# Query square sums in the DeltaNet stage: TensorE transposes squared on ScalarE in place of GpSimd squares and matmuls with a column of ones

## The chip, the cores and the metric

The kernel runs on one core of a Trainium2 chip. Its time is the device time of one execution in microseconds (us). Two numbers are used: the median of several runs, and the span of one profiled execution, from its first to its last instruction. The profile tells what each engine did in that one execution: PE is TensorE (matmuls, with PEld its weight loads), DVE is VectorE, ACT is ScalarE, POOL is GpSimd, SP is SyncE, which issues DMAs.

## The reference

One step of a decoder with two layers: a gated DeltaNet layer with a dense channel mixer, then a sliding-window attention layer with an expert mixer. 512 prompt tokens and 8 sample tokens pass through both. The change touches only the DeltaNet mixer of the prompt, and there the norm of the queries:

```python
def l2_norm(x):
    xf = x.astype(jnp.float32)
    return xf * lax.rsqrt(jnp.sum(xf * xf, axis=-1, keepdims=True) + EPS)
...
    q = l2_norm(q.reshape(Bn, T, A_HEADS, A_DK)) * (A_DK ** -0.5)
    k = l2_norm(k.reshape(Bn, T, A_HEADS, A_DK))
...
        o = (jnp.einsum('bhck,bhkv->bhcv', qi * jnp.exp(gi)[..., None], S)
             + jnp.einsum('bhij,bhjv->bhiv', attn, v_new))
...
    o = rms_norm(o, o_norm) * jax.nn.silu(zf)
```

The output of a token is linear in its query, so the norm of the query can be applied late: the kernel computes with unnormed queries and folds the sum of their squares into the norm of the output. That sum, one number for each token and head, is what is computed in another way here.

## The kernel before

The whole program is written out by engine, with semaphores between the engines. Its stages follow each other: input projection, the DeltaNet stage (`delta_phase`, from about 218 to 440 us of the span), output projection, dense mixer, attention, experts.

`delta_phase` goes through the 512 prompt tokens in NCH = 4 chunks of C = 128. The 8 heads are two groups, g = 0 and 1, of HL = 4 heads. Almost every step exists twice, once for each group, and is one instruction over 4 heads, or 4 matmuls. Every engine runs through its steps in the order in which the code lists them. The loop over chunks n inverts a triangular matrix in five levels (s = 2, 4, 8, 16, 32, two sets of 64x64 matmuls each, with ScalarE's copy of Y between them and VectorE's subtraction behind them), and between the levels stand steps that prepare chunk n + 1 ("prep") and steps that carry the state of chunk n - 1 on ("chain"). A class `Lane` counts the steps: `done(ins, who, n, step)` makes an instruction raise a semaphore, `after(eng, n, who=step)` makes an engine wait until that step is done.

PSUM has 8 banks, 4 for each group. Bank 3 of a group, `bank(g, 3)`, is used for one preparation step after another: decay matmuls, key transposes (`k_tok`), key scores (`kk`), query scores (`qk`), value transposes (`v_tok`), and last the square sums of the queries (`ssq`). Before the decay matmuls of the next chunk may write the bank, PE waits for VectorE's step `bq`, which reads the sums.

The path of the square sums of chunk n in the kernel before:

- GpSimd, `squares` (L803, tensor_tensor on L805): the queries `tokens(0, g, n)` times themselves into the buffer `SQ`, 128x512 for each group, issued early, behind the level s = 2 of the chunk before.
- PE, `query_sums` (L951 to L955): behind `solve_keys` and ahead of `recall`, for each of 4 heads a matmul with that head's squares as weights and one column of ones as the moving operand, result 128x1.
- VectorE, `queries` (L1368): scales the queries in place by the decay; it has to come after whatever reads the unscaled queries. Then `query_sums` (L1377): `bq` = (sum + EPS) * EPS * DK, read from PSUM, 128x4. Then `new_values` (L1394), two instructions for each group that wait for PE's `recall`.

Who waits for `bq`: PE's `decay` of the next chunk (L928), VectorE's own `sums_out`, and for the last chunk (n = NCH - 1) PE's `sample_scores` (L1054), which waits for `bq` of group 0 on L1057 because it writes that group's bank 3. `sample_scores` is a long run of small matmuls for the sample tokens, placed behind `recall` of chunk 2, ahead of the last chunk's levels.

In the trace, buffers have the names of the memory that they lie in: VectorE's `tt` helper is L1337, PE's transposes are L902 (`turn`), its 128x128 products L907 (`full`), its 64x64 products L913 (`blocks`). `SQ` of group 0 and 1 is `over_w_hi` and `over_w_lo`, the queries, keys and values are `qkv`, the small factors `delta_small`, the constant tile with identity and ones is `cst`, PSUM is `P`.

Of the kernel before, what the change touches and what calls it, by code (L numbers as in the profile page):

```python
# [17 lines left out]
ALU = mybir.AluOpType  # L18
# [9 lines left out]
AH, DK = 8, 128  # L28
# [657 lines left out]
def delta_phase(nc, c, io, L, sp_next):  # L686
# [17 lines left out]
    by_level = lambda *names: [f"{name}{s}" for s in LEVELS for name in names]  # L704
    prep, inv, chain = ([Lane(c, f"{what}{g}", steps) for g in range(2)] for what, steps in (
        ("prep", {"pe": ["decay", "k_tok", "kk", "qk", "v_tok", "ssq"],
                  "act": ["e_last", "e_left", "e_tok", "e_row", "k_copy", "e_attn", "sq_k", "root"],
                  "dve": ["left", "diff", "LT", "c", "attn", "VP", "q_dec", "bq"],
                  "pool": ["sq_q", "mask", "LT"]}),
        ("inv", {"pe": ["E1"] + by_level("Y", "XW") + ["Y64", "W64"],  # L710
                 "act": by_level("Y") + ["Y64", "F11", "F22", "F12"],
                 "dve": ["W1", "X1"] + by_level("XW"),
# [56 lines left out]
    with nc.Block() as block:  # L769
# [21 lines left out]
        def _(pool):  # L791
# [8 lines left out]
                prep[g].done(nc.gpsimd.affine_select(out=big("AT", g, n), in_=big("AT", g, n), compare_op=ALU.is_ge, fill=low, base=0,  # L800
                                                     pattern=[[0, HL], [1, C]], channel_multiplier=-1), "pool", n, "mask")

            def squares(g, n):  # L803
                prep[g].after(pool, n - 1, pe="ssq")
                prep[g].done(nc.gpsimd.tensor_tensor(big("SQ", g), tokens(0, g, n), tokens(0, g, n), ALU.mult), "pool", n, "sq_q")  # L805

            def scale(g, n):
                prep[g].after(pool, n, dve="c")
                LTc, LT12, cc = big("LTc", g), big("LT12", g, n), small("c", g, n)
# [43 lines left out]
                nc.gpsimd.tensor_tensor(k_mask[:, k], k_row[:, k].unsqueeze(1).broadcast_to([128, TS, 128]),  # L853
                                        cols(c, CPLACE, TS).unsqueeze(2).broadcast_to([128, TS, 128]), ALU.mult).then_inc(s_masked, 1)

            for step in (squares, mask, scale):
                for g in both:
                    step(g, 0)
            for s in (1, 2):
# [2 lines left out]
            for n in range(NCH):  # L862
                more, last = n + 1 < NCH, n == NCH - 1
                for s in LEVELS:
                    if s < 32:
                        for g in both:
                            part(g, n, 2 * s)
                    if more and s == 2:
                        for g in both:
                            squares(g, n + 1)  # L870
                    if more and s == 4:
                        for g in both:
                            mask(g, n + 1)
                    if s == 8:
                        for g in both:
                            decay_state(g, n)
                    if n == 0 and s == 16:
                        pool.wait_ge(edge_stored, 48)
                        for pad in pads:
                            nc.gpsimd.memset(pad, 0.0).then_inc(s_cleared, 1)  # L880
                    if n == 1:
                        fade_sample(LEVELS.index(s))
                    if n == 2 and s < 16:
                        fade_sample(5 + LEVELS.index(s))
                    if last and s >= 16:
                        mask_keys(s // 32)
                if more:
                    for g in both:
                        scale(g, n + 1)
                        part(g, n + 1, 1)  # L890
                if n:
                    for g in both:
                        weigh_F(g, n)
                if more:
                    for g in both:
                        part(g, n + 1, 2)

        @block.tensor
        def _(pe):
# [49 lines left out]
                prep[g].done(turn(bank(g, 3), tokens(2, g, n)), "pe", n, "v_tok")  # L949

            def query_sums(g, n):  # L951
                prep[g].after(pe, n, dve="VP", pool="sq_q")
                for h in range(HL):
                    ins = pe.matmul(c.P[:, 4 * g + 3, h:h + 1], big("SQ", g)[:, h], ones[:, 0:1], start=True, stop=True)
                prep[g].done(ins, "pe", n, "ssq")  # L955

            def first(g, n):
                inv[g].after(pe, n, pool="E1")
# [216 lines left out]
        def _(act):  # L1175
# [30 lines left out]
            def key_root(g, n):  # L1206
                prep[g].after(act, n, act="sq_k")
                prep[g].done(nc.scalar.activation(small("ssk", g, n), small("ssk", g, n), ACT.Sqrt, bias=cols(c, CEPS, 1)),
                             "act", n, "root")

            def level(g, n, s):
                inv[g].after(act, n, pe=f"Y{s}")
                inv[g].done(copy(big("Y", g), half(g, 0, 0)), "act", n, f"Y{s}")
# [34 lines left out]
            def edges(part):  # L1248
                act.wait_ge(edge_turned, part + 1)
                copy(edge_rows[:, part * 512:(part + 1) * 512], c.P[0:11, (4, 5, 6, 0, 1, 2)[part]]).then_inc(edge_read, 1)  # L1250
# [34 lines left out]
                    step(g, 0)  # L1285
            for part in range(3, 6):
                edges(part)
            for n in range(NCH):
                more, last = n + 1 < NCH, n == NCH - 1
                for s in LEVELS:  # L1290
                    for g in both:
                        level(g, n, s)
                    if more and s == 2:
                        for g in both:
                            decays(g, n + 1)
                    if n == 0 and s == 2:
                        nc.scalar.activation(L.s_decay[:], L.gb_sample[:, 0:AH * TS], ACT.Exp).then_inc(s_decays, 1)
                    if s == 4 and n:
                        for g in both:
                            square_out(g, n - 1)  # L1300
                    if more and s == 8:
                        for step in (keys, mask):
                            for g in both:
                                step(g, n + 1)
                    if more and s == 16:
                        key_sums(0, n + 1)
                    if s == 16 and n:
                        for g in both:
                            root_out(g, n - 1)
                    if more and s == 32:  # L1310
                        key_sums(1, n + 1)
                        for g in both:
                            key_root(g, n + 1)
                    if n == 0 and s == 4:
                        sample_rows()
                    if last and s == 2:
                        sample_take()
                    if last and s == 4:
                        sample_squares()
                for g in both:  # L1320
                    join(g, n)
                if n == 0:
                    sample_roots()
                for g in both:
                    corners(g, n)
                if n:
                    for g in both:
                        solve_keys(g, n)
            for g in both:
                square_out(g, NCH - 1)  # L1330
            for g in both:
# [3 lines left out]
        def _(dve):  # L1335
# [30 lines left out]
                prep[g].done(tt(big("AT", g, n), bank(g, 3), big("AT", g, n), ALU.mult), "dve", n, "attn")  # L1366

            def queries(g, n):  # L1368
                prep[g].after(dve, n, pool="sq_q")
                prep[g].done(tt(tokens(0, g, n), tokens(0, g, n), big("ER", g), ALU.mult), "dve", n, "q_dec")  # L1370

            def values(g, n):
# [2 lines left out]
                prep[g].done(tt(big("VP", g, n), bank(g, 3), per_head(small("ssk", g, n)), ALU.mult), "dve", n, "VP")  # L1375

            def query_sums(g, n):  # L1377
                prep[g].after(dve, n, pe="ssq")
                prep[g].done(nc.vector.tensor_scalar(small("bq", g, n), c.P[:, 4 * g + 3, 0:HL], EPS, EPS * DK, ALU.add, ALU.mult),
                             "dve", n, "bq")  # L1380

            def first(g, n):
# [110 lines left out]
            for n in range(NCH):  # L1493
# [40 lines left out]
                    if last and s == 32:  # L1534
                        sample_update(0)
                if more:
                    for step in (query_scores, first, values, queries, query_sums):
                        for g in both:
                            step(g, n + 1)
                if last:  # L1540
# [1 line left out]
                        sample_update(q)  # L1542
                for g in both:
                    new_values(g, n)
            sample_update(5)
            for g in both:
                add_state(g, NCH - 1)
# [1670 lines left out]
```

## Time and profile before

| what | us |
|---|---|
| median of 3 runs | 1588.41 (1588.24 to 1590.96) |
| the profiled execution | 1588.98 |
| its span | 1587.2 |
| PE busy | 1479.2 (93%) |
| DVE busy | 900.5 (57%) |
| ACT busy | 648.6 (41%) |
| POOL busy | 208.7 (13%) |

1.8 us of the profiled execution lie outside its span, and it is 0.57 us longer than the median. Busy times count what an engine executes, not its waits. PE is busy nearly always, so its steps set the time as long as it doesn't stand waiting; the other engines matter where PE waits for them. The granted clock of TensorE is 1.00 where it runs at 2.4 GHz and 0.50 where it runs at 1.2 GHz.

### The profile page before, as it was taken

To read this page: it belongs to the slowest core of one execution; us is meant where nothing else is said; L and a number is where in the kernel's file an instruction comes from. 1 tells how busy PE (TensorE), PEld (TensorE's weight loads), DVE (VectorE), ACT (ScalarE), POOL (GpSimd) and SP (SyncE) were. 2 spreads that over 40 slices of the span, in tenths; PEclk is the share of its full clock that TensorE was granted. 3 is DMA by queue.
4 is the path that set the end of the run, shared out by engine and by line. 5 is a ranking of instruction groups with operands and counts; after the bars stand their busy time and mean duration, and the time that the engine had idled before them with its cause. 6 is when DMAs were issued, how large, how long until landed. Compare 5 with 4: busy or idle time off the path is not lost. (4 is left out here: it accounts for less than half of the span.)

```text
span 1587.2 us, 31920 instructions
## 1 busy us (share of the span) xinstructions
PE 1479.2 (93%) x13294; PEld 1320.5 (83%) x13294; DVE 900.5 (57%) x1197; ACT 648.6 (41%) x1108; POOL 208.7 (13%) x217
## 2 busy tenths in 40 slices
PE   6999989899889999999999998879879999999994
PEld 6999978889889999999999997458867777777773
DVE  5676534755465443444444754543366777676776
ACT  5343534442143222222232413552434565665661
POOL 0111024554011000000011100220011000000002
PEclk8999999999889999999999997889879999999997
DMA  6678240000352323231334530005137888888886
GB/s 177 226 267 280 78 120 2 2 2 3 107 156 72 106 79 106 79 103 57 91 91 131 151 103 21 1 1 134 72 121 240 287 289 294 290 295 268 272 284 239
DMA packets 169741, 226.13 MB, mean 142 GB/s; under 512 B 11272, under 2 KB 134689, under 8 KB 169545
## 3 DMA queue, kind: packets, MB, share of 16 engines
q1 hardware_dynamic: 160246, 191.44, 38.7%
q0 software_dynamic: 8512, 30.48, 5.3%
q10 hardware_dynamic: 862, 2.50, 0.4%
q8 instruction: 88, 1.44, 0.4%
q14 instruction: 33, 0.27, 0.1%
HBM read 188.78 MB, written 37.88 MB: 143 GB/s over the span
## 5 line engine op out<-in xcount | busy, mean ns | idle before, releaser
L276 DVE TENSOR_TENSOR w_lo<-w_raw,w_hi 128x2048 fp32r<-128x2048 f32 (+1 forms) x71 | 153.9, 2172 | 91.4 <-ACT w_hi L268 91.4
L268 ACT ACTIVATE w_hi<-w_raw 128x2048 fp32r<-128x2048 f32 (+1 forms) x71 | 128.1, 1810 | 124.0 <-PE P L221 118.5
L221 PE MATMUL P<-xf_hi,w_hi 128*128 128x260 f32 x704 | 141.8, 282 | 2.0 <-DVEq L1764 1.2
L221 PE MATMUL P<-xf_hi,w_lo 128*128 128x260 f32 x704 | 141.9, 283 | 0.0
L221 PE MATMUL P<-xf_lo,w_hi 128*128 128x260 f32 x704 | 141.7, 283 | 0.0
L221 PEld LDWEIGHTS P<-xf_hi,w_hi 128*128 128x128 f32 x704 | 108.5, 188 | 2.6 <-issue 1.4
L221 PEld LDWEIGHTS P<-xf_hi,w_lo 128*128 128x128 f32 x704 | 108.5, 188 | 0.0
L221 PEld LDWEIGHTS P<-xf_lo,w_hi 128*128 128x128 f32 x704 | 108.2, 188 | 0.0
L221 PE MATMUL P<-xa_hi,w_hi 128*128 128x260 f32 x512 | 104.1, 285 | 2.7 <-DVE xa_lo L319 2.7
L221 PE MATMUL P<-xa_hi,w_lo 128*128 128x260 f32 x512 | 104.1, 285 | 0.0
L221 PE MATMUL P<-xa_lo,w_hi 128*128 128x260 f32 x512 | 103.9, 285 | 0.0
L2095 PE MATMUL P<-w_hi,xb_hi 128*128 128x512 f32 x344 | 102.6, 401 | 0.0
L1848 DVE TENSOR_TENSOR w_lo<-raw_more_moe,w_hi 128x1024 fp32r<-128x1024 f32 x64 | 77.1, 1223 | 42.6 <-ACT w_hi L1842 41.9
L1848 DVE TENSOR_TENSOR w_lo<-w_raw,w_hi 128x1024 fp32r<-128x1024 f32 x64 | 77.1, 1223 | 25.8 <-ACT w_hi L1842 24.4
L1842 ACT ACTIVATE w_hi<-raw_more_moe 128x1024 fp32r<-128x1024 f32 x64 | 66.1, 1054 | 44.6 <-DMA raw_more_moe<-in_moe_w_gu_dram 19.1
L221 PEld LDWEIGHTS P<-xa_hi,w_hi 128*128 128x128 f32 x512 | 80.0, 191 | 2.8 <-issue 2.8
L1842 ACT ACTIVATE w_hi<-w_raw 128x1024 fp32r<-128x1024 f32 x64 | 67.0, 1059 | 33.1 <-DMA w_raw<-in_moe_w_gu_dram 18.2
L221 PEld LDWEIGHTS P<-xa_hi,w_lo 128*128 128x128 f32 x512 | 79.9, 191 | 0.0
L221 PEld LDWEIGHTS P<-xa_lo,w_hi 128*128 128x128 f32 x512 | 79.7, 190 | 0.0
L2095 PEld LDWEIGHTS P<-w_hi,xb_hi 128*128 128x128 f32 x344 | 62.0, 188 | 19.1 <-issue 6.2
L221 PE MATMUL P<-f_hi,w_hi 128*128 128x260 f32 x352 | 70.9, 283 | 0.0
L221 PE MATMUL P<-f_hi,w_lo 128*128 128x260 f32 x352 | 70.8, 282 | 0.0
(553 smaller groups left out, 3320.5 us busy)
## 6 DMA issues: line engine op xcount, KB each, us to landing
raw_more_moe<-in_moe_w_gu_dram SPq DMA_DIRECT2D x64, 512.0 KB, 5.3
w_raw<-in_moe_w_gu_dram SPq DMA_DIRECT2D x64, 512.0 KB, 5.4
w_raw<-in_dense_w_gu_dram SPq DMA_DIRECT2D x44, 512.0 KB, 4.5
expert_out<-zeros POOLq DMA_DIRECT2D x40, 512.0 KB, 4.1
w_raw<-in_a_w_in_dram SPq DMA_DIRECT2D x32, 512.0 KB, 5.0
raw_more_moe<-in_moe_w_down_dram SPq DMA_DIRECT2D x32, 512.0 KB, 4.8
w_raw<-in_moe_w_down_dram SPq DMA_DIRECT2D x32, 512.0 KB, 4.7
w_raw<-in_dense_w_down_dram SPq DMA_DIRECT2D x16, 384.0 KB, 4.0
```

Of the source, the lines that this page charges most:

```text
L221: ins = nc.tensor.matmul(out[:, b], w, x[:, b * HALF:(b + 1) * HALF], start=(first and n == 0), stop=(last and n == 2))
L268: ins = nc.scalar.activation(hi, raw, ACT.Copy)
L276: ins = nc.vector.tensor_tensor(lo, raw, hi.bitcast(F32), ALU.subtract)
L1842: nc.scalar.activation(self.hi[m % 6], self.raw[s], ACT.Copy).then_inc(self.hi_done, 1)
L1848: nc.vector.tensor_tensor(self.lo[m % 6], self.raw[m % len(self.raw)], self.hi[m % 6].bitcast(F32), ALU.subtract).then_inc(self.lo_done, 1)
L2095: ins = pe.matmul(c.P[:, bank + b], a[:, t], x[:, b * 512:(b + 1) * 512], start=(t == 0 and x is w_hi and a is hi), stop=(t == KT - 1 and ...
```

## The change

The squares on GpSimd and the matmuls with ones go away. In their place PE transposes the queries of the chunk (4 transposes for each group, into bank 3, token on the partitions), and ScalarE takes the transposes from PSUM and squares them, with its accumulator adding each row up: 4 activations for each group, which write the sum into the small tile `bq`. VectorE then works on that small tile.

```diff
-                  "act": ["e_last", "e_left", "e_tok", "e_row", "k_copy", "e_attn", "sq_k", "root"],
+                  "act": ["e_last", "e_left", "e_tok", "e_row", "k_copy", "e_attn", "sq_k", "root", "sq_q"],
-                  "pool": ["sq_q", "mask", "LT"]}),
+                  "pool": ["mask", "LT"]}),
...
@block.gpsimd
-            def squares(g, n):
-                prep[g].after(pool, n - 1, pe="ssq")
-                prep[g].done(nc.gpsimd.tensor_tensor(big("SQ", g), tokens(0, g, n), tokens(0, g, n), ALU.mult), "pool", n, "sq_q")
-
...
-            for step in (squares, mask, scale):
+            for step in (mask, scale):
...
-                    if more and s == 2:
-                        for g in both:
-                            squares(g, n + 1)
...
@block.tensor
             def query_sums(g, n):
-                prep[g].after(pe, n, dve="VP", pool="sq_q")
-                for h in range(HL):
-                    ins = pe.matmul(c.P[:, 4 * g + 3, h:h + 1], big("SQ", g)[:, h], ones[:, 0:1], start=True, stop=True)
-                prep[g].done(ins, "pe", n, "ssq")
+                prep[g].after(pe, n, dve="VP")
+                prep[g].done(turn(bank(g, 3), tokens(0, g, n)), "pe", n, "ssq")
...
@block.scalar
+            def query_sums(g, n):
+                prep[g].after(act, n, pe="ssq")
+                for h in range(HL):
+                    ins = nc.scalar.activation(big("SQ", g)[:, h], bank(g, 3)[:, h], ACT.Square, accum_out=small("bq", g, n)[:, h:h + 1])
+                prep[g].done(ins, "act", n, "sq_q")
+
...
+            for g in both:
+                query_sums(g, 0)
             for n in range(NCH):
...
                 if n:
                     for g in both:
                         solve_keys(g, n)
+                if more:
+                    for g in both:
+                        query_sums(g, n + 1)
...
@block.vector
             def queries(g, n):
-                prep[g].after(dve, n, pool="sq_q")
+                prep[g].after(dve, n, pe="ssq")
...
             def query_sums(g, n):
-                prep[g].after(dve, n, pe="ssq")
-                prep[g].done(nc.vector.tensor_scalar(small("bq", g, n), c.P[:, 4 * g + 3, 0:HL], EPS, EPS * DK, ALU.add, ALU.mult),
+                prep[g].after(dve, n, act="sq_q")
+                prep[g].done(nc.vector.tensor_scalar(small("bq", g, n), small("bq", g, n), EPS, EPS * DK, ALU.add, ALU.mult),
...
-                    for step in (query_scores, first, values, queries, query_sums):
+                    for step in (query_scores, first, values, queries):
                         for g in both:
                             step(g, n + 1)
...
                 for g in both:
                     new_values(g, n)
+                if more:
+                    for g in both:
+                        query_sums(g, n + 1)
```

For chunk 0, VectorE's order stays as it was (`query_sums` directly behind `queries`); for chunks 1 to 3 it moves behind `new_values` of the chunk before.

VectorE at the end of the chunk n = 2, before. The `qkv` rows are `queries`, the L1379 rows are `query_sums` (`delta_small_2628` is group 0, `2629` group 1), the four rows behind them are `new_values`, the last is the addition to the state:

```order
L1337 TENSOR_TENSOR qkv<-qkv,delta_own 128x4x128 [waits prep0_pool]
L1337 TENSOR_TENSOR qkv<-qkv,over_w_lo 128x4x128 [waits prep1_pool]
L1379 TENSOR_SCALAR delta_small_2628<-P 128x4 [waits prep0_pe]
L1379 TENSOR_SCALAR delta_small_2629<-P 128x4 [waits prep1_pe]
L1337 TENSOR_TENSOR delta_own<-P,delta_small_2628 128x512 [waits chain0_pe]
L1337 TENSOR_TENSOR delta_own<-P,delta_small_2628 128x512 [waits prep0_act,chain0_pe]
L1337 TENSOR_TENSOR over_w_lo<-P,delta_small_2629 128x512 [waits chain1_pe]
L1337 TENSOR_TENSOR over_w_lo<-P,delta_small_2629 128x512 [waits prep1_act,chain1_pe]
L1337 TENSOR_TENSOR delta_own<-delta_own,P 128x512 [waits chain0_pool,chain0_pe]
```

The same place after the change, where VectorE's helper is L1339 and `query_sums` L1381:

```order
L1339 TENSOR_TENSOR qkv<-qkv,delta_own 128x4x128 [waits prep0_pe]
L1339 TENSOR_TENSOR qkv<-qkv,over_w_lo 128x4x128 [waits prep1_pe]
L1339 TENSOR_TENSOR delta_own<-P,delta_small_2628 128x512 [waits chain0_pe]
L1339 TENSOR_TENSOR delta_own<-P,delta_small_2628 128x512 [waits prep0_act,chain0_pe]
L1339 TENSOR_TENSOR over_w_lo<-P,delta_small_2629 128x512 [waits chain1_pe]
L1339 TENSOR_TENSOR over_w_lo<-P,delta_small_2629 128x512 [waits prep1_act,chain1_pe]
L1381 TENSOR_SCALAR delta_small_2628<-delta_small_2628 128x4 [waits prep0_act]
L1381 TENSOR_SCALAR delta_small_2629<-delta_small_2629 128x4 [waits prep1_act]
L1339 TENSOR_TENSOR delta_own<-delta_own,P 128x512 [waits chain0_pool,chain0_pe]
```

The two `bq` rows have moved behind the four of `new_values` and wait for ScalarE; `queries` waits for PE and no longer for GpSimd.

PE at the same place after the change. The L895 rows are the new transposes, L1005 is `recall`, L1049 and L1056 are the first instruction and the body of `sample_scores`:

```order
L895 MATMUL P<-cst,qkv 128x128 [waits prep0_dve]
L895 MATMUL P<-cst,qkv 128x128 x3
L895 MATMUL P<-cst,qkv 128x128 [waits prep1_dve]
L895 MATMUL P<-cst,qkv 128x128 x3
L1005 MATMUL P<-delta_front,delta_own 128x128 [waits chain0_dve,chain0_act]
L1005 MATMUL P<-delta_front,delta_own 128x128 x3
L1005 MATMUL P<-delta_front,over_w_lo 128x128 [waits chain1_dve,chain1_act]
L1005 MATMUL P<-delta_front,over_w_lo 128x128 x3
L1049 MATMUL P<-cst 128x512 [waits prep0_dve,sample_faded,sample_padded]
L1056 MATMUL P<-s_state,over_raw 8x128 x128
```

The transposes stand where the matmuls with ones stood, and the order on PE is the same otherwise; L1049 still waits for a VectorE step of group 0's preparation, which is `bq` of chunk 3.

## Rows read from the trace of the kernel before

**Rows 1.** The page: busy time by engine, and the granted clock in 40 slices.

```profile
PE 1479.2 (93%) x13294; PEld 1320.5 (83%) x13294; DVE 900.5 (57%) x1197; ACT 648.6 (41%) x1108; POOL 208.7 (13%) x217
PEclk8999999999889999999999997889879999999997
```

**Rows 2.** Timeline, PE, chunk 1 to 2: start us, busy us, instruction, [idle before].

```profile
319.00 1.04 PE L902 MATMUL P<-cst,qkv 128*128 128x128 f32 x8
319.96 0.68 PE L964 MATMUL P<-cst,over_w_hi 64*64 64x64 f32 x16
...
322.93 0.95 PE L954 MATMUL P<-cst,over_w_hi 128*128 128x1 f32 x8
...
324.63 1.14 PE L1014 MATMUL P<-delta_own 128*128 128x128 f32 x8
...
327.85 1.13 PE L907 MATMUL P<-delta_own 128*128 128x128 f32 x8
...
329.71 1.95 PE L932 MATMUL P<-cst,G_tok 128*128 128x128 f32 x16
```

**Rows 3.** Timeline, the same stretch on DVE, POOL and ACT.

```profile
322.89 0.68 DVE L1337 TENSOR_TENSOR qkv<-qkv,delta_own 128x512 f32<-128x512 f32 x1
...
323.17 0.99 POOL L824 TENSOR_TENSOR over_w_lo<-over_pair,levels 128x256 f32<-128x256 f32 x1 [0.16 <-PE P L907]
323.49 1.22 DVE L1337 TENSOR_TENSOR qkv<-qkv,over_w_lo 128x512 f32<-128x512 f32 x1
...
325.81 1.29 DVE L1337 TENSOR_TENSOR delta_own<-P,delta_small 128x512 f32<-128x512 f32 x2 [0.84 <-PE P L1014]
...
327.32 0.85 ACT L1177 ACTIVATE over_pair<-P 128x256 f32<-128x256 f32 x2 [3.60 <-PE P L913]
```

**Rows 4.** Timeline, chunk 2 to 3, PE and DVE around `sample_scores`.

```profile
366.81 0.95 PE L954 MATMUL P<-cst,over_w_hi 128*128 128x1 f32 x8
...
368.52 0.34 DVE L1379 TENSOR_SCALAR delta_small<-P 128x4 f32<-128x4 f32 x2
...
369.69 1.29 DVE L1337 TENSOR_TENSOR delta_own<-P,delta_small 128x512 f32<-128x512 f32 x2 [0.84 <-PE P L1014]
370.48 1.12 PE L1058 MATMUL P<-cst 1*128 1x512 f32 x2
...
371.53 7.17 PE L1065 MATMUL P<-s_state,over_raw 128*8 128x128 f32 x256
```

**Rows 5.** Timeline, chunk 0 to 1, PE and ACT.

```profile
279.09 1.05 PE L954 MATMUL P<-cst,over_w_hi 128*128 128x1 f32 x8 [1.62 <-DVE delta_own L1337]
...
281.69 0.85 ACT L1177 ACTIVATE over_pair<-P 128x256 f32<-128x256 f32 x2 [7.38 <-PE P L913]
...
282.22 2.05 PE L907 MATMUL P<-delta_own 128*128 128x128 f32 x8
...
285.61 1.95 PE L932 MATMUL P<-cst,G_tok 128*128 128x128 f32 x16
```

**Rows 6.** Timeline, PE before chunk 0's levels.

```profile
239.87 1.05 PE L954 MATMUL P<-cst,over_w_hi 128*128 128x1 f32 x8 [2.03 <-DVE delta_own L1337]
...
242.34 1.12 PE L913 MATMUL P<-over_w_hi,delta_own 64*64 64x64 f32 x16
```

**Rows 7.** Timeline, ACT: first and last of 8 squares with accumulator from PSUM.

```profile
292.06 0.27 ACT L1238 ACTIVATE delta_own<-P 128x128 f32<-128x128 f32 x1
...
293.97 0.26 ACT L1238 ACTIVATION_READ_ACCUMULATOR over_w_lo<-P 128x1 f32 x1
```

**Rows 8.** Busy time by stretch: us, then busy (count) by engine, PE clock, DMA share, GB/s.

```profile
242.00:244.00 2.00, 2.00 (x34) 1.99 (x34) 0.16 (x1) 0.38 (x1) 1.99 (x3) 0.50 0.00 0
282.00:284.00 2.00, 1.89 (x12) 1.81 (x9) 1.62 (x3) 1.74 (x3) 2.00 (x2) 0.50 0.04 8
306.00:308.00 2.00, 0.73 (x20) 0.74 (x22) 2.00 (x4) 0.22 (x2) 0.51 (x1) 1.00 0.00 0
```

**Rows 9.** Timeline, PE, inside chunk 1.

```profile
307.27 0.68 PE L913 MATMUL P<-over_w_hi,delta_own 64*64 64x64 f32 x16 [2.28 <-DVE over_w_hi L1337]
```

## The prediction

> **What bounds the kernel now.** I read the page first: PE is busy for 93% of the span, at a clock near full [rows 1], so a step that PE no longer makes is a gain as long as PE doesn't wait for something new. Then I read the timeline of the DeltaNet stage from one square-sum step to the next, on all engines. There are four such places: before the levels of chunk 0, and at the ends of chunks 0, 1 and 2. The reader is to look there for three things: how long PE takes from the start of the square-sum matmuls to its next step, who reads the bank behind it, and what else PE is about to wait for. At the ends of chunks 1 and 2, PE goes from L907 through L954 to L1014 without a gap [rows 2]: it is the bound there. At the end of chunk 0 and before chunk 0 it starts L954 late, because VectorE's values come late (1.62 and 2.03 us of waiting) [rows 5, 6]; the change doesn't touch that. GpSimd is busy 13% of the time [rows 1], and none of its squares holds up PE, so what it loses is worth nothing by itself.
>
> **The change part by part.**
>
> *PE.* The 8 matmuls with ones of both groups appear as 16 passes and take PE from 322.93 to 324.63, 1.70 us [rows 2]. Eight transposes of 128x128 (the values' own, L902) take it from 319.00 to 319.96, 0.96 us for both groups, in one pass each [rows 2]. So each place gives back 1.70 - 0.96 = 0.74, about 0.75 us, where PE is the bound. That an operation with 128 moving columns is cheaper than one with a single column is what the rows say: what both pay is the weight load, and the matmul in fp32 pays it twice. The Trainium skill, "TensorE: Matmul & The Clock Gate", Part 4: PE-mode transpose, gives about 275 ns for a 128x128 transpose inside a kernel; if each took that in sequence, eight would take 2.2 us, and each place would lose 0.5 us instead. The trace speaks against that reading: the busy time of one overlaps the next.
>
> *GpSimd.* Eight squares of about 1 us go. They stand beside other work; worth zero, and at the ends of chunks the next E products may start a little earlier, which nobody waits for.
>
> *ScalarE.* Eight squares with accumulator from PSUM take from 292.06 to 294.23, 2.17 us for both groups [rows 7]. They stand behind `solve_keys` and ahead of the copy of Y of the first level, which `level_two` and `add_state` on PE wait for.
>
> *End of chunk 1.* ScalarE has been free since 327.32 - 3.60 = 323.72 [rows 3]; the first transposes are done by about 323.5; the squares run from 323.75 to 325.9. The Y copy is wanted at 327.32 - 0.75 = 326.57. It is covered with 0.65 us to spare. VectorE: `queries` starts at 322.89 now [rows 3], ahead of L954 on PE; in future it waits for the transposes, until about 323.6 and 324.1. Its two instructions then meet GpSimd's E products. Where they met before, the second took 1.22 us and not 0.68, and GpSimd's 0.99 [rows 3]. If the two alternate, as there, `queries` ends at about 325.8, and the four instructions of `new_values`, which start at 325.81 now [rows 3] at some 0.6 us each, end near 328.3; the two `bq` follow until 328.6 (0.34 us for both [rows 4]). PE wants `bq` for the decay matmuls at 329.71 - 0.75 = 328.96 [rows 2], and `new_values` for L907 at 327.85 - 0.75 = 327.10, when group 0's first is done. Nothing new waits: -0.75 us.
>
> *End of chunk 2.* The same, until `sample_scores`. It waits for `bq` of group 0. Now `bq` is done by 368.86 and PE starts L1058 at 370.48, right behind `recall` [rows 4]. After the change `bq` stands behind `new_values`, and that waits for `recall`. By the rows: PE would be ready at 370.48 - 0.75 = 369.73. VectorE can start `new_values` at 369.69 - 0.75 = 368.94 if `queries` is over by then, and at about 369.7 if it alternates with GpSimd as above. Four instructions of some 0.6 us and `bq` (0.17) make 2.6 to 2.7 us: `bq` of group 0 is ready at 371.6 or at 372.4. L1058 starts then, 1.1 or 1.9 us later than now. All of it is on the path: nothing else is under way, and PE has `sample_scores` (7.17 us) next [rows 4]. I take the upper value, +1.9, because at the same place one chunk earlier the rows show the encounter with GpSimd. The Trainium skill, "SBUF — State Buffer", section "SBUF: two separate sides", states that a VectorE operation with two SBUF inputs and a GpSimd operation lock each other out for the whole of an instruction. The 1.22 us of the row agree; by that rule the place costs +1.9, and without it +1.1.
>
> *End of chunk 0.* The levels' first step would start 0.75 us earlier, but ScalarE comes later. VectorE's instructions of this size follow each other by 0.6 us (323.49 - 322.89 [rows 3]), so group 1's transposes have their values at 279.09 + 0.6 = 279.7, and the squares run from about 279.85 to 282.0, and the Y copy, now at 281.69 [rows 5], starts at 282.0. L907, now at 282.22, waits for it until 282.4. So +0.1 us here, where the 0.75 could have been: the cover is gone by 1 us. L907 then runs, now as before, at half clock: 3.39 us for both groups from 282.22 to 285.61 [rows 5], with a granted clock of 0.50 [rows 8], against 329.71 - 327.85 = 1.86 us at full [rows 2]. If that half-speed stage went away, 1.5 us would be gained. PE has had a wait of 1.62 us and one-column matmuls just before it [rows 5]; afterwards it would have the same wait, real transposes, and a new wait of about a microsecond. I can't tell from the rows, and leave the stage as it is.
>
> *Before chunk 0.* L954 starts at 239.87 and the levels at 242.34, 2.47 us later [rows 6]; the transposes of group 0 start at the same time, those of group 1 when its values are there, 0.6 us later at 240.47, and end half a microsecond later: the levels start at 240.95, 1.4 us earlier. The clock is at 0.50 at 242 [rows 8]. If it comes back at the same moment as before, the 1.4 us pulled ahead run at half speed and 0.7 are kept; if the whole stage shifts, 1.4. ScalarE's squares (2.17 us from 240.5) end near 242.7, and the `bq` for the decay matmuls is ready about then; PE has two sets of 64x64 matmuls until then. I take -1.4.
>
> *Sum:* -1.4 + 0.1 - 0.75 + 1.9 = -0.15 us. Its bounds: -0.15 - 0.8 (no encounter in chunk 2) = -0.95, and +0.7 (prologue at half) = +0.55. Behind the stage PE runs on as before: what is gained or lost moves everything behind it. Against the profiled execution (1588.98) that is 1588.8, and against the median, which is 0.57 lower, 1588.41 - 0.15 = 1588.3 us.
>
> **The rivals.**
>
> *Faster: half-speed stages shorten.* PE now has two such stages beside the changed steps, one around 242 and one around 282 [rows 8]. Each is worth about 1.5 us by the difference above (3.39 against 1.86). One gone: 1588.3 - 1.5 = 1586.8. Both, or one and a later one that starts at another moment: 1585.3. For it: real matmul work takes the place of one-column matmuls. Against it: the waits ahead of them stay. Chance 0.22 for one, 0.09 for two or more.
>
> *The wait of `sample_scores` doesn't bind.* If VectorE got through `new_values` sooner, the third place would give -0.75 and not +1.9: 1588.3 - 2.65 = 1585.7. Against it: the order of VectorE puts four instructions that need `recall` ahead of `bq`, and `recall` is what PE finishes last. Chance 0.05.
>
> *Transposes no cheaper.* If transposes of queries cost what the matmuls did, the chunk 1 place gives 0, the place before chunk 0 about 0.7 less, and the third still ends with `bq`: 1588.3 + 0.75 + 0.7 + 0.2 = 1590.0. Against it: the same instruction on the same tile shape is in the trace. Chance 0.04.
>
> *Slower: the new wait brings the clock down under `sample_scores`.* PE would stand for 2 to 2.7 us just ahead of 7.17 us of matmuls [rows 4]. If the clock fell to half and stayed there for all of it, up to 7.2 us would be added: 1595.5; if for half of it, 3.6: 1591.9. It decides from the point at which the wait is long enough for the clock to fall. Against it: a wait of 2.28 us ended at 307.27 [rows 9], and the clock is 1.00 in 306 to 308 with PE busy 0.73 of 2 us [rows 8]. Chance 0.09, and 0.07 for more than 3.2 us.
>
> **How the numbers follow.** Forecast 1588.3 with a chance of 0.51 (its own range 1587.3 to 1589.5), the others as given. A measurement of this kernel tells about 0.2% (3.2 us) from no change: below 1585.2, above 1591.6. Faster needs two stages of half speed gone, or one and the missing wait: 0.10. Slower needs the clock under `sample_scores`: 0.07. The rest, 0.83, is within. The range from 1585.3 to 1591.0 takes in one stage more or less, both bounds of the third place and the execution-to-execution spread of the runs before (2.7 us).
>
> **What would show it.** In the profile after: from the first transposes of the queries to L1005 about 0.95 us (right) or 1.7 (wrong); on ScalarE, eight squares in about 2.2 us directly behind the WK copies; between L1005 and L1049 a wait of 1.9 to 2.7 us for VectorE's small tile, the largest single change; at the end of chunk 0 the Y copy behind the squares without a gap; in the stretches at 242 and 282 the clock. The prediction would be wrong if that wait were missing or the clock under L1056 were 0.50.

## The result and the profile after

The kernel after took 1593.11 us (median of 20 runs, 1587.61 to 1597.48), the kernel before 1589.01 us (median of 20, 1586.46 to 1590.96). The ratio is 1.0026, with a 95% interval of 1.0017 to 1.0034: slower, by some 4 us. The profiled execution of after took 1594.36 us, with a span of 1592.6 us; that of before 1588.98, with a span of 1587.2.

The page of after, busy time by engine and granted clock, beside [rows 1]:

```profile
PE 1480.7 (93%) x13262; PEld 1318.2 (83%) x13262; DVE 901.8 (57%) x1197; ACT 656.0 (41%) x1172; POOL 200.2 (13%) x209
PEclk8999999999789999999999997789879999999997
```

PE's busy time rose by 1.5 us although it runs 32 passes fewer: the modelled time of a matmul grows with a lower clock. The answer is in the places that the change touches. The timeline of after, PE (start us, busy us, instruction, idle before in brackets), ahead of chunk 0's levels, beside [rows 6]:

```profile
239.79 1.25 PE L895 MATMUL P<-cst,qkv 128*128 128x128 f32 x8 [2.03 <-DVE delta_own L1339]
240.97 1.07 PE L906 MATMUL P<-over_w_hi,delta_own 64*64 64x64 f32 x16
...
245.59 0.68 PE L906 MATMUL P<-over_pair,over_w_hi 64*64 64x64 f32 x16
```

The levels start at 240.97 and not at 242.34, 1.4 us sooner. The clock, too, is back sooner (0.88 in 244 to 246 us, where it was 0.50, and 0.53 in 246 to 248): `level_two` starts at 245.59, 2.35 us ahead of before. The end of chunk 0, on PE, DVE and POOL, beside [rows 5]:

```profile
276.56 1.90 POOL L843 TENSOR_TENSOR s_state<-s_state,s_decay 128x1024 f32<-128x1024 f32 x1
276.59 0.67 DVE L1339 TENSOR_TENSOR over_w_lo<-P,delta_small 128x512 f32<-128x512 f32 x1
276.72 1.25 PE L895 MATMUL P<-cst,qkv 128*128 128x128 f32 x8 [1.62 <-DVE delta_own L1339]
277.42 1.59 DVE L1339 TENSOR_TENSOR qkv<-qkv,delta_own 128x512 f32<-128x512 f32 x1 [0.15 <-PE P L895]
...
278.68 0.91 POOL L820 TENSOR_TENSOR delta_own<-over_w_hi,levels 128x256 f32<-128x256 f32 x1 [0.22 <-PE P L906]
...
278.93 1.21 DVE L1339 TENSOR_TENSOR qkv<-qkv,over_w_lo 128x512 f32<-128x512 f32 x1
...
280.06 1.28 DVE L1339 TENSOR_TENSOR delta_own<-P,delta_small 128x512 f32<-128x512 f32 x2
280.79 1.16 PE L900 MATMUL P<-delta_own 128*128 128x128 f32 x8 [1.74 <-DVE delta_own L1339]
...
281.99 2.07 PE L900 MATMUL P<-over_w_lo,over_w_hi 128*128 128x128 f32 x8
...
286.49 0.68 PE L906 MATMUL P<-over_pair,over_w_hi 64*64 64x64 f32 x16
```

`fade_sample(0)` on GpSimd (L843, the fading of the sample state), 1.90 us long, stands on top of the first of VectorE's two `queries`, and the E product behind it (L820) on top of the second: they take 1.59 and 1.21 us in place of 0.68 each. `new_values` comes late, PE waits 1.74 us, and the clock goes to half behind that wait (2.07 us for a step that takes 1.06 at full). The lead is down to 1.00 us. The end of chunk 1, beside [rows 2] and [rows 3]:

```profile
322.01 1.04 PE L895 MATMUL P<-cst,qkv 128*128 128x128 f32 x8
322.88 1.06 PE L1005 MATMUL P<-delta_own 128*128 128x128 f32 x8
...
327.88 1.95 PE L925 MATMUL P<-cst,G_tok 128*128 128x128 f32 x16
```

Eight transposes take PE 0.87 us. The place goes as forecast: the decay matmuls start 1.83 us ahead of before where the values' transposes were 0.92 ahead. The end of chunk 2, beside [rows 4]:

```profile
364.99 1.04 PE L895 MATMUL P<-cst,qkv 128*128 128x128 f32 x8
365.86 1.06 PE L1005 MATMUL P<-delta_front,delta_own 128*128 128x128 f32 x8
366.75 1.06 PE L1005 MATMUL P<-delta_front,over_w_lo 128*128 128x128 f32 x8
370.27 1.55 PE L1049 MATMUL P<-cst 1*128 1x512 f32 x2 [2.46 <-DVE delta_small L1381]
371.76 10.00 PE L1056 MATMUL P<-s_state,over_raw 128*8 128x128 f32 x256
```

and VectorE in the same stretch:

```profile
366.44 1.21 DVE L1339 TENSOR_TENSOR qkv<-qkv,over_w_lo 128x512 f32<-128x512 f32 x1
367.58 1.28 DVE L1339 TENSOR_TENSOR delta_own<-P,delta_small 128x512 f32<-128x512 f32 x2
368.78 1.27 DVE L1339 TENSOR_TENSOR over_w_lo<-P,delta_small 128x512 f32<-128x512 f32 x2
369.97 0.23 DVE L1381 TENSOR_SCALAR delta_small<-delta_small 128x4 f32<-128x4 f32 x2
```

PE stands for 2.46 us ahead of `sample_scores`, since `bq` is behind the four instructions of `new_values`. Then `sample_scores` takes 10.00 us for its large step, not 7.17. The windows of after give PE's busy time with its count, the granted clock, DMA share and GB/s:

```profile
368.00:370.00 2.00, 0.00 (x0) 1.00 0.00 0
370.00:372.00 2.00, 1.73 (x10) 0.69 0.03 8
372.00:374.00 2.00, 2.00 (x44) 0.50 0.00 0
374.00:376.00 2.00, 2.00 (x47) 0.50 0.00 0
376.00:378.00 2.00, 2.00 (x52) 0.60 0.00 0
```

Behind a stretch in which PE did nothing, the clock is at its lower level (1.2 GHz) for most of the step: 44 matmuls in 2 us in place of the 84 of full speed. The next level step starts at 381.99, against 378.94 before: 3.05 us behind. The remaining 2.3 us of the 5.4 between the two profiled executions come later, where no instruction changed. 1.4 of them come before the output projection, which starts at 447.83 against 443.37; there the half-speed stretches lie otherwise (granted clock 0.67 in 400 to 426 us, before 0.74).

### The profile page after: what moved, and what is told of

The parts are those of the page before. It is cut to its first block and busy times, and to the rows that moved or that the text cites. A ratio compares the mean times of both kernels' runs of the same rounds, so it can differ in the third digit from the quotient of the medians.

```text
span 1592.6 us, 31904 instructions
## 1 busy us (share of the span) xinstructions
PE 1480.7 (93%) x13262; PEld 1318.2 (83%) x13262; DVE 901.8 (57%) x1197; ACT 656.0 (41%) x1172; POOL 200.2 (13%) x209
```

## The experiments

Two theories were set against each other. A: the loss is the wait ahead of `sample_scores` and the clock under it. B: the loss comes from half-speed stretches elsewhere, which have nothing to do with the wait. All ratios are to the kernel before, timed beside the experiment.

**One part undone: `bq` of group 0 early.**

```diff
@@ after, VectorE, end of a chunk
+                if n + 1 == NCH - 1:
+                    query_sums(0, n + 1)
                 for g in both:
                     new_values(g, n)
-                if more:
+                if n + 1 == NCH - 1:
+                    query_sums(1, n + 1)
+                elif more:
                     for g in both:
                         query_sums(g, n + 1)
```

> The kernel after, but for the last chunk VectorE makes the small tile bq of group 0 ahead of new_values, and that of group 1 behind it. Only the place of two small instructions changes. Theory A (the kernel after loses because sample_scores waits for bq and PE's clock falls under it): the wait of 2.46 us ahead of sample_scores goes, its first step takes about 7 us again and not 10.0, and no stretch between 371 and 378 us is at 0.50. Wait and clock together give 2 to 2.4 + 3.0 = 5 to 5.5 us: 1593.1 - 5.3 = about 1587.8. Rival B (the loss is the sum of the half-speed stages later on, which have nothing to do with this place): at most the wait comes back, 1591 or more. Rival C (the clock falls under sample_scores for other reasons than the wait): wait gone, clock still 0.50, about 1591.

Measured: 1587.69 us, ratio 0.9993 (0.9981 to 1.0004), against 1.0026 for after. Its timeline:

```profile
367.46 1.09 PE L1049 MATMUL P<-cst 1*128 1x512 f32 x2 [0.60 <-DVE delta_small L1381]
368.49 7.17 PE L1056 MATMUL P<-s_state,over_raw 128*8 128x128 f32 x256
```

The place of one instruction of 128x4 is worth 5.2 us by the ratios (0.33% of 1589). Theory A's sum is met; B is out as the main cause.

**One part alone: `bq` late in the kernel before.**

```diff
@@ before, VectorE, end of a chunk
-                    for step in (query_scores, first, values, queries, query_sums):
+                    for step in (query_scores, first, values, queries) + (() if n + 1 == NCH - 1 else (query_sums,)):
...
                 for g in both:
                     new_values(g, n)
+                if n + 1 == NCH - 1:
+                    for g in both:
+                        query_sums(g, n + 1)
```

> The kernel before, but for the last chunk VectorE makes the two small tiles bq behind new_values instead of ahead of it. This is the one part of the change that moves the wait; transposes, ScalarE's squares and the missing GpSimd squares are not in it. Theory A: sample_scores waits 1.7 to 2.5 us for bq and the clock falls to 0.50 under it for about 3 us: 1589.0 + 2 + 3 = about 1594. Rival B (the loss sits elsewhere): 1589 to 1590. If the wait is there and the clock stays at 1.00: about 1591.

Measured: 1594.23 us, ratio 1.0033 (1.0020 to 1.0046). Without a transpose of the queries or a square of them on ScalarE in it, this kernel loses what after loses:

```profile
373.22 1.09 PE L1058 MATMUL P<-cst 1*128 1x512 f32 x2 [1.84 <-DVE delta_small L1379]
374.25 8.84 PE L1065 MATMUL P<-s_state,over_raw 128*8 128x128 f32 x256
```

**The wait filled with work.** This kernel does more than after: 22 transposes that nobody uses.

```diff
@@ after, PE
                 if n == NCH - 2:
+                    for _ in range(22):
+                        pe.transpose(c.P[:, 0, 0:128], ident, ident)
                     sample_scores()
```

> The kernel after with 22 transposes of the identity added on PE between recall and sample_scores of the last chunk, whose result is used by nobody: they fill the wait of 2.46 us with work (0.11 us each by the rows, 2.4 us together). Theory A (the clock falls because PE stands still in that wait): sample_scores starts when it did, to 0.2 us, its first step takes about 7 and not 10 us, the stretch behind it is at 1.00: about 3 us less than after, 1590. Rival (the clock falls whatever PE does in the wait): same time as after, 1593, with 0.50 under sample_scores.

Measured: 1589.94 us, ratio 1.0001 (0.9990 to 1.0012).

```profile
365.99 1.06 PE L1005 MATMUL P<-delta_front,over_w_lo 128*128 128x128 f32 x8
366.88 2.56 PE L1155 MATMUL P<-cst 128*128 128x128 f32 x22
369.51 1.09 PE L1049 MATMUL P<-cst 1*128 1x512 f32 x2
370.53 7.17 PE L1056 MATMUL P<-s_state,over_raw 128*8 128x128 f32 x256
```

`sample_scores` starts as late as in after (2.46 us behind the end of `recall` in both), yet adding useless work makes the kernel faster by 0.25%, 4 us by the ratios and 3.2 by the medians. So the loss splits: 1 to 2 us are the wait (1.3 by the ratios of this experiment and the first, 1.9 by the brackets 2.46 and 0.60), 3 to 4 the clock behind it, and that clock falls because PE stood still.

**Half of the wait filled.** The same edit with `range(11)`.

> The kernel after with 11 transposes of the identity added on PE between recall and sample_scores of the last chunk, not 22: the wait ahead of sample_scores is about 1.2 us, and sample_scores starts when it did, since VectorE's bq sets that. Theory (the fall needs the long wait): clock 1.00 under sample_scores, its first step 7.2 us, time as with 22 of them: 1590. Rival (any wait at this moment lets it fall): 0.50 under sample_scores for about 3 us, 1592 to 1593.

Measured: 1592.21 us, ratio 1.0013 (1.0001 to 1.0025), between the two theories. A fall in one execution of five, below, accounts for only some 0.3 us of it; the interval overlaps that of the filled wait, and where the rest comes from stays open. Five executions of this kernel were profiled, in all of them with a wait of 1.25 or 1.26 us; four have 7.17 us for the large step, and one, the fourth, has 8.84:

```profile
368.84 1.09 PE L1049 MATMUL P<-cst 1*128 1x512 f32 x2 [1.26 <-DVE delta_small L1383]
369.86 8.84 PE L1056 MATMUL P<-s_state,over_raw 128*8 128x128 f32 x256
```

> The kernel with 11 filling transposes, unchanged, in one more execution. Its profiled execution had a wait of 1.25 us and clock 1.00 under sample_scores, and a span of 1586.2, while its median is 1592.2. Theory 1: a wait of 1.25 us never lets the clock fall there, and the slow executions lose elsewhere: first step 7.2 us again. Theory 2: it falls in the executions above 1591 or so: first step 8.8 to 10 us, if this execution is one of them.

> The kernel with 11 filling transposes again, a third profiled execution. If a wait of 1.25 us doesn't let the clock fall there: first step of sample_scores 7.2 us whatever the time of the execution. If it does in slow executions: 8.8 to 10 us in one above 1591.

> The same kernel, a fourth execution: 7.2 us at any time of the execution (no fall behind 1.25 us), or 8.8 to 10 us in one above 1591.

> The same kernel, a fifth execution: 7.2 us at any time of the execution (no fall behind 1.25 us), or 8.8 to 10 us in one above 1591.

Measured: 1590.28, 1592.12, 1588.87 and 1590.53 us. The expectation that the fall would show in an execution above 1591 was wrong: it came in the one of 1588.87, and the one of 1592.12 lost its time elsewhere. A short wait lets the clock fall now and then; the total of one execution doesn't tell whether it did.

**The kernels after and before, once more.**

> The kernel after, unchanged, profiled in one more execution, since its executions lie between 1587.6 and 1597.5 us. Theory S (steady): the wait of 2.46 us ahead of sample_scores and 0.50 under it for 2.8 to 3.3 us are in every execution; the spread comes from half-speed stages elsewhere. Theory D (by the execution): the wait is there each time, but the clock falls under sample_scores only in some, and the first step takes 7.2, 8.8 or 10.0 us.

> The kernel after, unchanged, a third profiled execution. Theory S: first step of sample_scores near 10.0 us again. Theory D: 7.2 to 10.0, unlike in the others.

> The kernel before, unchanged, in one more profiled execution, to see how far the places of the half-speed stages move without any edit. Expected if they are tied to the kernel's waits: first step of sample_scores 7.2 us at 1.00; half-speed stages at 240 to 248 and 282 to 285 us as in the first profile, within one step of some 3.4 us.

Measured: 1597.47 and 1589.16 us for after, 1590.66 for before. The two executions of after at `sample_scores`, the first and then the second:

```profile
369.83 2.04 PE L1049 MATMUL P<-cst 1*128 1x512 f32 x2 [2.46 <-DVE delta_small L1381]
371.80 9.42 PE L1056 MATMUL P<-s_state,over_raw 128*8 128x128 f32 x256
```

```profile
368.51 1.09 PE L1049 MATMUL P<-cst 1*128 1x512 f32 x2 [2.46 <-DVE delta_small L1381]
369.54 8.84 PE L1056 MATMUL P<-s_state,over_raw 128*8 128x128 f32 x256
```

Wait and fall are in each execution; how long the fall lasts is not: 1.67 us are lost in the second (8.84 - 7.17), 3.2 in the first (9.42 - 7.17 and 2.04 - 1.09). All profiled executions by the length of the wait:

| wait ahead of `sample_scores`, us | executions | large step, us |
|---|---|---|
| none or filled (before twice, 22 transposes, and two kernels below) | 5 | 7.17 in all |
| 0.59 to 0.60 (`bq` early; both edits, twice) | 3 | 7.17 in all |
| 1.25 or 1.26 | 5 | 7.17 in four, 8.84 in one |
| 1.84 (`bq` late in before) | 1 | 8.84 |
| 2.46 (after three times, and `fade_sample` later) | 4 | 10.00, 9.42, 8.84, 8.84 |

**GpSimd's `fade_sample(0)` later.**

```diff
@@ after, GpSimd, fade_sample
                 if h == 0:
+                    prep[1].after(pool, 1, dve="q_dec")
                     pool.wait_ge(s_loaded, 16 * AH)
```

> The kernel after, but GpSimd's fade_sample(0), one instruction of 128 x 1024, waits for VectorE's queries of chunk 1 to be over (both groups) before it starts. Theory: at the end of chunk 0, queries takes 0.68 us an instruction again and not 1.59 and 1.21, new_values starts about 1.4 us earlier, and PE's wait ahead of the first add_state step (1.74 us) falls by 0.8 to 1.4: 0.8 to 1.4 us less than after, 1592, if the half-speed stages later stay as they are. Rival: ScalarE's copy of Y, which now stands behind the squares, ends that wait anyway: 0 to 0.3 us less.

Measured: 1590.23 us, ratio 1.0013 (1.0001 to 1.0025), so 2.1 us less than after by the ratios, more than the 0.8 to 1.4 expected; the interval overlaps that of after (1.0017 to 1.0034). VectorE and GpSimd at the end of chunk 0:

```profile
277.56 0.69 DVE L1340 TENSOR_TENSOR qkv<-qkv,delta_own 128x512 f32<-128x512 f32 x1 [0.15 <-PE P L896]
...
278.17 0.68 DVE L1340 TENSOR_TENSOR qkv<-qkv,over_w_lo 128x512 f32<-128x512 f32 x1
...
278.94 1.90 POOL L844 TENSOR_TENSOR s_state<-s_state,s_decay 128x1024 f32<-128x1024 f32 x1 [2.19 <-DVE qkv L1340]
```

Where more than the wait may come back is seen over many executions. From PE's first transpose of the queries to `level_two`, in microseconds:

| kernel, executions | wait ahead of `add_state` | half speed | stretch |
|---|---|---|---|
| no `fade_sample` edit, 7 of 10 | 1.73 or 1.74 | behind the wait | 9.46 to 9.77 |
| no `fade_sample` edit, 3 of 10 | 0.40 to 0.43 | ahead of it, under the first levels | 7.83 to 7.85 |
| with the edit, 2 of 4 | 0.34 to 0.39 | ahead of it | 7.78 to 7.81 |
| with the edit, 2 of 4 | 1.07 to 1.08 | none | 7.14 to 7.15 |

Without the edit a half-speed stretch stood at this place each time, mostly behind the wait, where all of it counts. With the edit none stood behind it in four executions. On average the stretch takes 9.07 us without the edit and 7.47 with it: 1.6 us, of which 0.7 are the wait (1.74 against 1.08) and the rest the clock.

**Both edits.**

> The kernel after with both edits: for the last chunk bq of group 0 ahead of new_values, and GpSimd's fade_sample(0) behind VectorE's queries of chunk 1. Theory 1 (each edit takes away a loss of its own): the first alone gave 1587.7; the second frees VectorE by 1.4 us at the end of chunk 0, of which PE can keep 0.5 to 1.4: 1586.3 to 1587.2. Theory 2 (what the second edit gave alone, 2.9 us, was mostly a shorter fall of the clock under sample_scores, which the first edit has removed already): 1587.7, as the first alone.

> The kernel with both edits (bq of group 0 early, GpSimd's fade_sample(0) late) timed again. If its gain stands: 1585 to 1587, ratio to before under 0.999. If it was luck of the first runs: 1587.5 or more.

Measured: 1585.79 us, ratio 0.9977 (0.9965 to 0.9990), and timed again 1586.18, ratio 0.9980 (0.9968 to 0.9991). Both are below either kernel: the change with two orders mended gains 3 us over before, where as made it loses 4. Against `bq` early alone the second edit gives another 0.13 to 0.16%, as it gave 0.13% against after. Each of these differences lies within the two intervals that it is taken from; that they repeat, and that the timelines show the same, speaks for theory 1 (1586.3 to 1587.2) over theory 2 (1587.7). One execution at the end of chunk 0:

```profile
280.76 1.13 PE L901 MATMUL P<-delta_own 128*128 128x128 f32 x8 [1.08 <-ACT over_pair L1169]
```

and its windows on PE, at full clock where after had 0.51 and 0.64:

```profile
282.00:284.00 2.00, 2.00 (x21) 1.00 0.04 8
284.00:286.00 2.00, 2.00 (x56) 1.00 0.00 0
```

What ends the wait here is ScalarE's copy of Y behind its squares, as the prediction had it.

**`bq` of group 0 between the two `queries`.**

```diff
@@ both edits, VectorE, last chunk (the call ahead of new_values goes)
                     for step in (query_scores, first, values, queries):
                         for g in both:
                             step(g, n + 1)
+                            if n + 1 == NCH - 1 and step is queries and g == 0:
+                                query_sums(0, n + 1)
...
-                if n + 1 == NCH - 1:
-                    query_sums(0, n + 1)
                 for g in both:
                     new_values(g, n)
```

> As the kernel with both edits, but bq of group 0 stands between VectorE's two queries instructions of the last chunk, not behind them. With bq behind them sample_scores still waited 0.60 us. Theory: ScalarE's squares of group 0 are done when queries of group 0 is, the 0.60 us wait goes, and new_values starts up to 0.2 us later, which the levels of the last chunk don't feel: 0.5 us less than the kernel with both edits. Rival: the earlier start of sample_scores moves the next steps onto new_values, which is not sooner: no difference.

Measured: 1587.09 us, ratio 0.9984 (0.9972 to 0.9995). The wait is gone:

```profile
365.71 1.12 PE L1050 MATMUL P<-cst 1*128 1x512 f32 x2
```

That is 0.62 us ahead of the 366.33 of both edits, and the span is the shortest of the profiled ones (1582.8 us), but the medians don't show it. Its gain over both edits stays open: half a microsecond is below what these runs tell apart.

**The change for chunk 0 alone.** In the kernel before, chunk 0 takes the new way (PE's transposes, ScalarE's squares, VectorE's `bq` from the small tile), chunks 1 to 3 the old one:

```diff
@@ before, PE, query_sums (and in the same manner on the other engines)
+                if n == 0:
+                    prep[g].after(pe, n, dve="VP")
+                    prep[g].done(turn(bank(g, 3), tokens(0, g, n)), "pe", n, "ssq")
+                    return
                 prep[g].after(pe, n, dve="VP", pool="sq_q")
```

> The kernel before with the change made for chunk 0 alone: there the queries' square sums come from transposes squared on ScalarE; in chunks 1 to 3 from GpSimd's squares and the column of ones, as before. Theory (what is gained before chunk 0 lasts): the levels of chunk 0 start 1.3 us earlier, and the half-speed stage there ends one stage sooner or not: 1.3 to 2.4 us less than before, 1586.6 to 1587.7. Rival (a lead is given back, since half-speed stages further on begin at other moments): 1588.5 to 1589.5 with the lead of 1.3 us or more still seen at 250 us in the profile.

Measured: 1588.44 us, ratio 0.9995 (0.9985 to 1.0005). In the profile the levels start 1.21 us behind the first transpose (before: 2.47), and `sample_scores` starts 2.4 us ahead of before (368.08 against 370.48). The time lies between the two theories, and the interval doesn't part them: of the 2.4 us, 0.8 (by the ratio) to 1.4 (by the medians) are seen in the whole.

## Why the prediction was wrong

1593.1 us lies above the range of 1585.3 to 1591.0. By its own steps, from the profiled executions:

| place | forecast, us | measured, us |
|---|---|---|
| ahead of chunk 0 | -1.4 | -2.35 (1.4 of shorter work, 1.0 of clock) |
| end of chunk 0 | +0.1 | +1.35 |
| end of chunk 1 | -0.75 | -0.91 |
| end of chunk 2, until `sample_scores` | +1.9 | +1.6 |
| under `sample_scores` | 0 (a rival: 3.6 or 7.2) | +3.3 |
| behind it | 0 | +2.3 |

Inside chunk 1 another 0.1 us was lost; the sum is the 5.4 us between the two executions. The medians lie 4.1 us apart.

*PE's step.* Right. Eight transposes take 0.87 us in place of 1.70. The figure of the Trainium skill ("TensorE: Matmul & The Clock Gate", Part 4: PE-mode transpose), about 275 ns, read in sequence, would have made it 2.2 us. The trace agrees with it as the duration of a single one (median 273 ns on L895); in a row each adds 0.11 us.

*Before chunk 0.* The shorter work is right; that the half-speed stretch there would shorten too was the prediction's faster rival (0.22), and that part of it came true. From the first instruction of the sums to `level_two` the three profiled executions with the old way for chunk 0 take 7.91 to 8.07 us, the 15 with the new way 5.63 to 5.80.

*ScalarE.* Right: 8 squares in 2.3 us (forecast 2.17), and the Y copy at the end of chunk 1 is not late.

*The new wait.* Right in place and size (2.46 us in the bracket, +1.6 net of PE's gain), with the encounter of `queries` and GpSimd (1.21 us) behind it.

*The clock behind the wait.* This is the step that failed: the sum has nothing for it, and it measured +3.3 us. Without it the median would be about 1589.8 us (an estimate, 1593.1 - 3.3), inside the range, and the kernel with the filled wait measured 1589.94. The prediction had the mechanism as a rival, with the chance 0.09, and set it aside because a wait of 2.28 us had left the clock at 1.00 [rows 8, 9]; even the rival's smaller price, 1591.9, lay outside the range. One row of one execution can't bear that. In the profile of after the same wait at the same place, 2.27 us, is followed by half speed:

```profile
306.27 1.12 PE L906 MATMUL P<-over_w_hi,delta_own 64*64 64x64 f32 x16 [2.27 <-DVE over_w_hi L1339]
```

```profile
306.00:308.00 2.00, 1.73 (x33) 0.50 0.00 0
```

All 18 profiled executions have a wait of 2.27 to 2.30 us at this place. In 8 of them a half-speed stretch begins there, at 304.9 to 307.3 us, in the wait or up to 1.1 us behind it; in 10 the clock stays. So behind a wait of this length it may stay or fall from one execution to the next; under `sample_scores`, behind 2.46 us, it fell in four of four. The price of the rival was near (3.6 against 3.3 measured); its chance was not.

*GpSimd's squares are worth nothing.* Wrong too: taking them away cost time at the end of chunk 0. The prediction had ScalarE's copy of Y end PE's wait there, for +0.1; it was VectorE's late `new_values` that ended it. The squares had waited for PE's square sums, and `fade_sample(0)` waited in line behind them. GpSimd in the kernel before:

```profile
280.22 1.51 POOL L805 TENSOR_TENSOR over_w_hi<-qkv 128x512 f32<-128x512 f32 x1 [1.25 <-PE P L954]
...
282.69 1.89 POOL L847 TENSOR_TENSOR s_state<-s_state,s_decay 128x1024 f32<-128x1024 f32 x1
```

At 282.69 it is clear of `queries`, which ran from 279.56. Without the squares it starts at 276.56 and holds `queries` up. The prediction checked who needed GpSimd's work, and not what stood behind it in the queue, nor what that would meet on its way. The Trainium skill, "SBUF — State Buffer", section "SBUF: two separate sides", has a VectorE operation with two SBUF inputs and a GpSimd operation that reads SBUF shut each other out for a whole instruction. The trace agrees: GpSimd's 276.56 + 1.90 = 278.46, and the first of `queries`, begun at 277.42, ends 0.55 us behind that, at 279.01; the E product ends at 278.68 + 0.91 = 279.59, and the second, begun at 278.93, ends 0.55 us behind that, at 280.14. The +1.35 is of one pair of executions. From the first instruction of the sums to `level_two` the four with the old way at this place take 8.22 to 9.85 us (mean 8.70), the ten of the table above without the `fade_sample` edit 7.83 to 9.77 (mean 9.07), so on average less is lost here than in this pair.

*Behind the stage.* The prediction carried the sum to the end unchanged. By their medians, after, `bq` early and the filled wait each end about 1 to 1.7 us worse against before than they stand at 380 us in their one profile. Which cause that has, beyond half-speed stretches that begin at other moments, no run settles.

## What to carry to other kernels

When an operation leaves a queue, look at what stood behind it and will now start sooner, and at whom it meets; here that cost about 2 us, at the edge of what the runs can tell. When a new wait lands on PE, price the long step behind it at half clock as well: a tiny operation that this step needs belongs ahead of the large ones on its engine, and here its place was worth 5 us. With both orders mended, the same change went from 4 us lost to 3 us gained.

## What the runs showed of the hardware

At `sample_scores` the clock fell behind a long wait more often than behind a short one: in none of 8 executions with 0.6 us or less, in 1 of 5 with 1.25, in 5 of 5 with 1.84 or 2.46. The length isn't all: inside chunk 1, 2.27 to 2.30 us let it fall in 8 of 18.

The same kernel lies up to 10 us apart from run to run, and the clock has a large part in it. Two executions of after, span and mean granted clock:

```profile
core 0: 1595.7 us, clock 0.945
```

```profile
core 0: 1587.4 us, clock 0.950
```

An estimate of the time lost to the clock is span times (1 - clock), taking a stretch at 0.50 to do half the work: 1595.7 x 0.055 = 87.8 us and 1587.4 x 0.050 = 79.4. The difference, 8.4, is as large as the 8.3 us between the spans, though the clock's last digit alone is worth 0.8 us on either side. For other pairs it is a part only: of the 20 runs of after, one had a span of 1595.4 us at 0.949 and one 1585.8 at 0.951, 3.7 of the 9.6 us between them.

Added transposes which nobody reads made a kernel 0.25% faster.
